# From the second out tile of each FFN phase on, the out product runs one token half after the other

## What is computed

```python
def _swiglu(u, w_in, w_out):
    h = u @ w_in
    a, b = h[..., :D_FF], h[..., D_FF:]
    return (jax.nn.silu(a) * b) @ w_out
```

## Time and profile before

| | |
|---|---|
| runs | 1880.62 us median of 3 (1880.25 to 1882.64) |
| profiled execution | 1879.91 us, of which the span from first to last instruction is 1878.1 us |
| TensorE granted clock, mean | 0.996 of 2.4 GHz |
| matmuls | 13850, as many weight loads |
| matmuls of the out tiles with j > 0 outside `last_half` | 7 phases x 7 tiles x 66 + 6 x 66 = 3630 |

### The profile page before, as it was taken

How to read it: one execution, slowest core, us unless ns; L and a number is a source line. 1 busy time by engine, 2 the same in 40 slices (tenths; PEclk the granted TensorE clock), 3 DMA queues, 4 the chain that set the end, 5 groups by cost and what they waited for, 6 DMA issues and landing times.

```text
span 1878.1 us, 34441 instructions
## 1 busy us (share of the span) xinstructions
PE 1855.2 (99%) x13850; PEld 1834.6 (98%) x13850; DVE 1251.5 (67%) x1999; ACT 866.9 (46%) x1518; POOL 329.5 (18%) x352
## 2 busy tenths in 40 slices
PE   8999999999999999999999999999999999999998
PEld 8999999998999999999999999999989999999998
DVE  7874487668884488679853886563546888548853
ACT  7552355347552355346532553232334665235532
POOL 2220122131220122132201221300010322012112
PEclk9999999999999999999999999999999999999999
DMA  8773576334763576347644763231113576357632
GB/s 207 166 149 105 128 167 148 108 85 95 166 147 108 127 167 150 107 107 165 146 131 102 171 141 101 86 102 68 57 45 103 117 169 152 108 120 167 135 93 82
DMA packets 116830, 234.71 MB, mean 125 GB/s; under 512 B 13184, under 2 KB 15248, under 8 KB 116672
## 3 DMA queue, kind: packets, MB, share of 16 engines
q1 hardware_dynamic: 77440, 160.59, 28.7%
q0 software_dynamic: 38208, 69.42, 22.5%
q10 hardware_dynamic: 1024, 2.49, 0.4%
HBM read 228.92 MB, written 3.53 MB: 124 GB/s over the span
## 4 chain that ended last, share of the span: by engine, by line
PE 93%; DVE 4%; ACT 2%; DMA 1%; issue 1%; DVEq 0%; ACTq 0%
PE ps L1850 49%; PE ps L1840 39%; DVE w_lo L1231 1%; PE ps L1895 1%; PE ps L2167 1%; PE ps L2233 0%; DVE u L1285 0%; DMA raw_z<-in_ffn_in 0%; PE ps L2170 0%; DMA x<-in_x 0%; PE ps L2032 0%; PE ps L2157 0%; DVE rstd L1302 0%; ACT w_hi L726 0%; PE ps L2142 0%
## 5 line engine op out<-in xcount | busy, mean ns | idle before, releaser
L1850 PE MATMUL ps<-u,w_hi 128*128 128x288 f32 x4928 | 984.0, 295 | 11.7 <-DVE w_lo L1231 4.5
L1850 PEld LDWEIGHTS ps<-u,w_hi 128*128 128x128 f32 x4928 | 790.6, 188 | 16.4 <-DVE w_lo L1231 9.4
L1850 PE MATMUL ps<-u,w_lo 128*128 128x288 f32 x2464 | 727.1, 295 | 0.0
L1850 PEld LDWEIGHTS ps<-u,w_lo 128*128 128x128 f32 x2464 | 462.6, 188 | 0.0
L1840 PE MATMUL ps<-h_hi,w_hi 128*128 128x288 f32 x1386 | 294.4, 293 | 0.0
L1840 PE MATMUL ps<-h_lo,w_hi 128*128 128x288 f32 x1386 | 294.3, 293 | 0.0
L1840 PE MATMUL ps<-h_hi,w_lo 128*128 128x288 f32 x1386 | 294.3, 293 | 0.0
L726 ACT ACTIVATE w_hi<-w_raw 128x768 fp32r<-128x768 f32 (+3 forms) x164 | 136.0, 836 | 316.6 <-PE ps L1840 240.2
L1231 DVE TENSOR_TENSOR w_lo<-w_raw,w_hi 128x768 fp32r<-128x768 f32 (+3 forms) x164 | 168.8, 1038 | 160.6 <-ACT w_hi L726 158.4
L1840 PEld LDWEIGHTS ps<-h_hi,w_lo 128*128 128x128 f32 x1386 | 220.4, 188 | 0.0
L1840 PEld LDWEIGHTS ps<-h_hi,w_hi 128*128 128x128 f32 x1386 | 220.3, 188 | 0.0
(11 more groups left out here) (268 smaller groups left out, 2123.5 us busy)
## 6 DMA issues: line engine op xcount, KB each, us to landing
raw_a<-in_ffn_in SPq DMA_DIRECT2D x132, 256.0 KB, 4.2
w_raw<-in_ffn_out SPq DMA_DIRECT2D x64, 384.0 KB, 3.2
raw_y<-in_ffn_in SPq DMA_DIRECT2D x88, 256.0 KB, 3.6
raw_x<-in_ffn_in SPq DMA_DIRECT2D x88, 256.0 KB, 2.7
raw_x<-in_ffn_in POOLq DMA_DIRECT2D x88, 256.0 KB, 6.5
raw_y<-in_ffn_in POOLq DMA_DIRECT2D x88, 256.0 KB, 4.9
raw_z<-in_ffn_in POOLq DMA_DIRECT2D x88, 256.0 KB, 5.1
w_raw<-in_ffn_out SPq DMA_DIRECT2D x64, 320.0 KB, 3.0
```

Of the source, the lines that this page charges most:

```text
L1850: mm = pe.matmul(dst, w, m, start=prod in ("M1", "M2", "M5") and kp == 0 and p == 0, stop=kp == KP - 1 and p == 2, skip_group_check=prod i ...
```

## The change

From tile j = 1 on, `ffn_out` puts the halves outermost: 33 matmuls of half 0 into bank b, then 33 of half 1 into bank b + 1. The wait for `lo_split` stays ahead of a unit's first matmul, which is in half 0; `unit_used` is counted by the unit's last matmul, which is now in half 1. Tile j = 0, which waits for each hidden tile, and `last_half` stay as they were. The number of matmuls and weight loads is the same.

```diff
-                    k = 0
-                    for s, size in enumerate(OUT_UNIT):
-                        u = f.unit(ph, "out", j, s)
-                        pe.wait_ge(lo_split, u + 1)
-                        for kk in range(size):
-                            if j == 0:
+                    if j == 0:
...
+                        continue
+                    for h in range(2):
+                        k = 0
+                        at = slice(h * HALF, (h + 1) * HALF)
+                        for s, size in enumerate(OUT_UNIT):
+                            u = f.unit(ph, "out", j, s)
+                            if h == 0:
+                                pe.wait_ge(lo_split, u + 1)
+                            for kk in range(size):
+                                for p, (w, m) in enumerate(passes(u, kk, h_hi[:, k, at], h_lo[:, k, at])):
+                                    mm = pe.matmul(ps[:, out_bank(j) + h, 0:HALF], w, m,
+                                                   start=k == 0 and p == 0, stop=k == PAIRS - 1 and p == 2)
+                                k += 1
+                            if h == 1:
+                                mm.then_inc(unit_used, 1)
```

More of the change, by code:

```diff
@@ L1944, in ffn_out @@
                         pe.wait_ge(x_ready, DT * (f.norm + 1) + j - 1)
-                    k = 0
-                    for s, size in enumerate(OUT_UNIT):
-                        u = f.unit(ph, "out", j, s)
-                        pe.wait_ge(lo_split, u + 1)
-                        for kk in range(size):
-                            if j == 0:
-                                pe.wait_ge(h_ready, base + k + 1)
[L1952 to L1955, removed]
+                    if j == 0:
[4 more added lines that the diff above has]
+                            for kk in range(size):
+                                pe.wait_ge(h_ready, base + k + 1)
+                                mm = block_mm(u, kk, (h_hi[:, k, :], h_lo[:, k, :]), out_bank(j),
+                                              k == 0, k == PAIRS - 1)
+                                k += 1
+                            mm.then_inc(unit_used, 1)
+                        continue
+                    for h in range(2):
+                        k = 0
+                        at = slice(h * HALF, (h + 1) * HALF)
+                        for s, size in enumerate(OUT_UNIT):
+                            u = f.unit(ph, "out", j, s)
+                            if h == 0:
+                                pe.wait_ge(lo_split, u + 1)
+                            for kk in range(size):
+                                for p, (w, m) in enumerate(passes(u, kk, h_hi[:, k, at], h_lo[:, k, at])):
+                                    mm = pe.matmul(ps[:, out_bank(j) + h, 0:HALF], w, m,
+                                                   start=k == 0 and p == 0, stop=k == PAIRS - 1 and p == 2)
+                                k += 1
+                            if h == 1:
+                                mm.then_inc(unit_used, 1)
             def ffn(f):
```

## The result

The changed kernel takes 1884.83 us (median of 21 runs, 1882.45 to 1891.31), the kernel of before 1882.03 us beside it (21 runs, 1877.63 to 1885.12). The ratio is 1.0018, 95% interval 1.0011 to 1.0025: slower by 3.4 us, between 2.1 and 4.7. The forecast was +7.0 us. The sign was right and the size was twice too large. So the question is which of the forecast's terms was too large.

A forecast was written before the change was run, and what follows sets the result against it. TensorE, busy for 99% of the span, was taken as the bound: matmul count times start-to-start distance. Spacing +6.0 us and later release +1.0 us gave +7.0 us, a forecast of 1887.5 us, range 1882 to 1891.5.

The forecast's parts named there:

- The spacing of the new form: Out tiles from j = 1: changed matmuls start 132.5 ns apart, as in `last_half`; +6.0 us over 3630 matmuls.
- The later release: First unit of an out tile released 2.0 us later; delays the add at two turns between stages, +1.0 us together.
- the subtraction 2.0 - 1.36 at the turn b to c: FFN b to FFN c: release delay less VectorE's wait before the add makes the add 0.6 us late; 0.6 counted.
- Six of the eight out stretches run at 130.0 ns, two at 133.3: Spacing of the old out stretches, read from one trace; gave 475.0 us before against 481.0 us after.
- Input stretches in another rhythm than before: One of the observations in the new profile that the forecast said would show it wrong; no size given.
- the distance hardly depends on the order: Rival: new out tiles settle at 131.4 ns, 1883.6 us, or input stretches gain what out tiles lose; chance 0.27.
- The second half of that rival: Four input stretches directly behind out stretches go from 132.2 to 131.4 ns, giving back 3.0 us: 1880.6 us.
- The faster side: Rival: runs in one bank without repeated weights let out-tile matmuls close up; at 129.0 ns, 1874.9 us; chance 0.06.
- wait for `lo_split`: Sign of being wrong: TensorE waiting for `lo_split` within a phase; the forecast held weights ready in time, at no cost.
- The price of the stall: Rival: later loads make TensorE wait on weights or DMA, 3.2 us at the longest, giving 1890.8 us; chance 0.07.
- the first rival: The rival that the distance hardly depends on the order: 1883.6 us, or 1880.6 if input stretches gain; chance 0.27.

The follow-up runs named there:

- e1_release_late: Kernel of before with its matmul order kept; only the release of an out tile's first unit moves from matmul 36 to 51: 1881.41 us, ratio 1.0001.
- e2_unitwise: Halves outermost inside each unit (18 and 18, then 15 and 15 matmuls), against the changed kernel's runs of 33: 1881.68 us, ratio 1.0002 to before.
- e8_h_plus_64: Kernel of before with h_hi and h_lo 64 bytes further in SBUF: 1881.4 us, ratio 1.0012.
- e12_runs_to_set_rhythm: Kernel of before with strictly alternating input operand starts, and halves outermost in out tiles 1 and 7 alone: 1895.31 us, ratio 1.0077.
- e3_h_plus_128: Changed kernel with h_hi and h_lo 128 bytes further in SBUF: 1883.45 us, ratio 1.0012 to the kernel of before.

## Why the prediction came out as it did

**The spacing of the new form: right.** The forecast took 132.5 ns from `last_half`; 132.4 was measured in all eight phases of both profiles, 133.3 and 131.5 by half. The term over the out stretches was +6.0 us; the first pair of profiles gives 556.3 - 550.0 = 6.3, the second 6.1.

**The later release: mechanism right at one turn, size too large.** Counted 1.0 us, measured 0.3 (e1_release_late, and every kernel with the late release). The step of this term that failed is the subtraction 2.0 - 1.36 at the turn b to c. It assumed that VectorE's wait shrinks by the whole delay of the release. In the profile of before VectorE was still busy with the operand of the next FFN when the two `w_hi` were done, and only then wrote `w_lo` at 827.99 and 828.60. So part of the 2.0 us went into its queue before it reached the wait: in e1_release_late the `w_lo` end at 830.0, just as the tile does. The wait before an operation isn't all the slack there is; the queue ahead of the producer has some too.

**The base of the comparison: one draw, taken for a constant.** "Six of the eight out stretches run at 130.0 ns, two at 133.3" was read from one execution and put into the sum as if the program fixed it. Four profiles of the old out tiles have 550.0, 549.8, 549.8 and 555.0 us of out stretches, the changed order 555.9 and 556.3. The difference is 6 us where two stretches are slow, and 1 where five are. The mean over the four is 551.2, so the change costs 4.9 us there and not 6.3. The rest of the span has a mean of 1326.0 in these four and of 1325.6 in the two of the changed kernel. Together +4.5 us by the profiles, against 3.4 (2.1 to 4.7) and 4.1 (2.4 to 5.6) by the two sets of runs.

Of the 2.5 us by which +7.0 exceeds this +4.5, then, 1.1 lie in the base and 0.7 in the release. The other 0.7 lies in the rest of the span, whose four values before reach from 1323.6 to 1328.1, and isn't explained. The 1.1 us hang on a single profile, the one with five slow stretches; without it the mean is 549.9 and the term of +6.0 is nearly right. That profile's rest is the lowest of the four: two of its input stretches ran at 131.1 ns, where each of the others had one. How often each rhythm comes in the runs that weren't profiled stays open.

**A sign of being wrong.** "Input stretches in another rhythm than before" came by the letter: the one of 107.23 us in the earlier trace rows took 108.13 in the changed kernel. The kernel of before took 108.13 for it in its own second profile, so this is another draw and not the change.

**The rivals.** That the distance hardly depends on the order is false: one order gave 130.0 or 133.3, the other 132.4. The second half of that rival, input stretches that gain, came with other kernels (e2_unitwise, e8_h_plus_64) and not with the change. The Trainium skill's rule, page "TensorE: Matmul & The Clock Gate", section "Wait — 56ns, not 53.3ns?", has the columns alone in it, and by it matmuls of 288 columns start an estimated 122.5 ns apart; the words "whatever order they stand in" are the forecast's reading of it. It isn't borne out here: no input or out stretch ran below 130.0, and the order made a difference of up to 3 ns. The same page, section "Step-by-step: what each phase is for", says that loading weights takes no SBUF read bandwidth from the running matmul. Shifting the weights alone cost 10 us, so on this kernel the two aren't independent, though no run shows by what path. The faster side didn't come, and no wait for `lo_split` came within a phase. The price of the stall was misread: the wait of 3.2 us stands at 17.63 us, at the start of the kernel, and has nothing to do with the load of 8.31 us, behind which TensorE waited 0.63 us. The time fell near the first rival's, for another reason than the one given there.

## What to carry to other kernels

In a kernel that TensorE fills, look at start-to-start distances by stretch before looking at waits. A difference of 3 ns in 130 between two stretches with the same instructions was here a state into which the engine fell anew, and one profile shows one draw of it. So base a forecast of less than 1% on several profiles. Where the kernel holds the new form of a loop anywhere, take its spacing there as the price: here it gave 132.5, and 132.4 was measured. And a loop can pass on a rhythm to the loop behind it: judge an order by both. The unitwise order had slower out tiles than the changed kernel and yet less time, by what it gave back in the input stretches.

## What the runs showed of the hardware that was not expected

- The distance between float32r matmuls of 288 columns depends on where their moving operands start, modulo 256 bytes. With the weights 128 past a multiple of 256: all at 0, 133.3 ns; all at 128, 131.6; in turn 0, 128: 130.0 or 133.3, in two stable rhythms, over up to 2,800 matmuls running, in one bank or two, with repeated weights or without. In the pattern 0, 128, 0: 132.2 or 131.1, also in two rhythms. At 64 and 192 in turn: 132.2.
- At one place, ahead of the second out stretch of FFN a, a wait of 0.3 to 0.6 us was followed by a slow out stretch of 528 matmuls in both profiles of the old order that had it, and a fast one followed in both that hadn't, 1.75 us less.
- The weights' start counts as well: with the rings at a multiple of 256 in place of 128 past one, the fast rhythm of the out tiles was not seen in any of the eight stretches, and the kernel was 0.53% slower.
- A run of 33 matmuls of half 1 was followed by the slow rhythm in strictly alternating stretches in all eight phases (e12_runs_to_set_rhythm), in two of which the tile before had been fast, and by 132.2 in the stretches of pattern 0, 128, 0 (the changed kernel). Runs of 15 were followed by 131.1 (e2_unitwise). With the halves' starts in the turn 128, 0, tile 0 was slow in all eight phases (e3_h_plus_128). Why a rhythm holds, and what sets it after a wait, stays open.
